# The first layer's prologue in quarters of the features: squares added on VectorE, roots by columns of tokens, first products in a new order

## The chip, the core and the metric

The kernel runs on one core of one Trainium2 chip. The metric is the device time of one execution in microseconds (us); the time given is the median of several executions. Its engines are TensorE (matrix products, PE in the rows, its weight loads PEld), VectorE (DVE), ScalarE (ACT), GpSimd (POOL) and SyncE (SP), each of which works through its own list of instructions in order; semaphores tie the lists together.

## What is computed

Two blocks run one after the other on 512 tokens of 1024 features. The change touches only the start of the first layer of the first block. Cut to that, the reference is:

```python
def rmsnorm(x, g):
    xf = x.astype(jnp.float32)
    y = xf * lax.rsqrt(jnp.mean(xf * xf, axis=-1, keepdims=True) + RMS_EPS)
    return (y * g.astype(jnp.float32)).astype(x.dtype)
def modulate(h, shift, scale):
    return h * (1 + scale) + shift
# first_block, layer 0: x is 512x1024, ctx 256x1024
shift, scale, gate = jnp.split(sc @ mod_w[l] + mod_b[l], 3, axis=-1)      # sc = silu(c)
hx = modulate(rmsnorm(x, norm_g[l]), shift[:, None], scale[:, None])
shift_c, scale_c, gate_c = jnp.split(scc @ mod_w[l] + mod_b[l], 3, axis=-1)   # scc = silu(c_ctx)
hc = modulate(rmsnorm(ctx, norm_g[l]), shift_c, scale_c)
# even mixer: z = h @ w_in, split into va, vg, ga, xb, gb
# conformer: u = va * sigmoid(vg), convolution, layernorm, silu, times silu(ga)
# recurrence: xb through a short convolution u; gates r, i from u; a scan; the context gives its start
```

## The kernel before

Everything is held feature-major: a tile is 128 features (partitions) by 512 tokens of x, or by 256 tokens of the context (`TC`), and there are `NT` = 8 tiles of features. A product runs in three passes over split numbers: `three` (L1781) issues w_hi times h_hi, w_hi times h_lo and w_lo times h_hi for one tile k, `blocks` runs over k. The weights come in chunks of 128x1024 in the order that `chunk_names` (L61) gives. Each chunk c passes through rings of `RING` = 4 buffers: a transfer into `raw` (SP's queue, the first ones ScalarE's), `w_hi` by ScalarE (`hi`, L473), `w_lo` by VectorE (`lo`, L1015). `ahead(name)` makes the part of the chunk `AHEAD` = 3 places further on. A product waits with `ready` for its w_lo (semaphore `lo`), and counts itself done on `mm`. The order of each engine is written out by hand in `act`, `dve`, `pe`, `sp` and `pool`; no planner moves anything.

The prologue has four parts.

1. Loads: on ScalarE's queue x in two halves, the context, then `modr` (shift and scale columns of `mod_w`) in four quarters of 2 MB each in the order `GROUPS`, three weight chunks ahead of the third quarter.
2. Roots: ScalarE squares the tiles (L530), VectorE adds them in pairs (`square_pair`, L1104), four matmuls with a matrix of ones (`first_sum`, L1834) sum over features and leave the sum on all partitions, ScalarE takes the root of 128x512 and 128x256, VectorE the reciprocals (L1053).
3. Conditioning: TensorE multiplies silu(c) by each quarter (`mod_rows`, L1819, 16 matmuls), ScalarE copies the rows out (`rows_copy`, L538), TensorE turns them into columns (`mod_columns`, L1827), VectorE makes gains out of them (`first_gains`, L1133 and L1136), once for each half of the features.
4. h: for each tile VectorE multiplies x, gain and reciprocal root (`first_tile`, L1144), ScalarE adds the shift and rounds (`first_high`, L544: `h_hi`, `hc_hi`), VectorE makes the low part (`first_low`, L1150).

`first_products` (L1849) then multiplies by halves: the context's product xc(0), then the gate vg(0) and the value va(0) together, tile by tile. Eight passes i follow: vg(i), va(i), xc(i+1) and gc(i), the last being the recurrence's gates of the context. For pass i ScalarE takes tanh of vg(i), and after gc(i) the gate functions (`head_gates`) and their roots; VectorE makes `U` (L1227), the short convolution (`head_conv`), the scan's inputs and the scan (`head_drive`, `head_scan`), and one column of the conditioning (`conditioning`, L1061) for later use. The low parts of the next chunks stand between them in the same list.

## Time and profile before

| | |
|---|---|
| time, median of 3 executions | 1636.33 us (1633.75, 1636.33, 1636.61) |
| profiled execution | 1635.51 us, its span 1634.2 us |
| granted TensorE clock, mean | 0.993 |
| busy: TensorE, VectorE, ScalarE | 1597.6, 978.5, 752.7 us |

The span is what the engines' records cover; the 1.3 us to the execution's own time lie around it. The granted clock is the TensorE clock that the chip allowed, as a share of full speed: 1.00 is 2.4 GHz, 0.50 is 1.2 GHz. In a timeline a row gives the start in us from the span's beginning, the duration, the engine, the source line, the operation with its output and inputs by name, and in brackets the idle time before it with what ended it. A row with x16 groups sixteen such instructions. Source lines are those of the kernel before.

### The profile page before, as it was taken

The numbers are of one execution on the slowest core, as the hardware profiler recorded it, in microseconds if no ns is written. First come the engines' busy times: TensorE is split into PE (matmuls) and PEld (weight loads), VectorE is DVE, ScalarE is ACT, GpSimd is POOL, SyncE is SP. The second block draws the span as 40 slices with busy tenths as digits, with TensorE's granted clock in tenths as the row PEclk, the third lists the DMA queues.
The fourth block names the chain that finished last, engine by engine and source line by source line (L and its number), as shares of the span: only waits on it lengthen the run. The fifth ranks groups of instructions, "written<-read, shape, count | busy, mean of one in ns | idle before, by whom it ended". The sixth has DMA issues, their size and how long they took to land.

```text
span 1634.2 us, 19145 instructions
## 1 busy us (share of the span) xinstructions
PE 1597.6 (98%) x7642; PEld 1272.4 (78%) x7642; DVE 978.5 (60%) x1421; ACT 752.7 (46%) x1050; POOL 23.7 (1%) x44
## 2 busy tenths in 40 slices
PE   5999999999999999999999989999999999999998
PEld 2888767677788888888878866787888888888886
DVE  5877778787886566645755544465456544444223
ACT  4788665755554333333355654345334333333212
POOL 0000000000000000000000000000000000000000
PEclk9999999999999999999999999999999999999999
DMA  9344456563233322333212211222223323223321
GB/s 390 128 144 170 154 194 190 192 193 128 92 102 103 103 92 90 103 104 96 94 54 91 68 62 52 90 78 77 91 90 103 103 91 103 91 94 99 103 90 52
DMA packets 54104, 185.75 MB, mean 114 GB/s; under 512 B 7392, under 2 KB 7392, under 8 KB 53120
## 3 DMA queue, kind: packets, MB, share of 16 engines
q1 hardware_dynamic: 47472, 152.70, 29.1%
q0 software_dynamic: 5104, 18.72, 3.6%
q10 hardware_dynamic: 1440, 13.11, 1.9%
q8 instruction: 60, 0.98, 0.2%
q14 instruction: 28, 0.23, 0.0%
HBM read 173.91 MB, written 2.10 MB: 108 GB/s over the span
## 4 chain that ended last, share of the span: by engine, by line
PE 89%; DVE 5%; ACT 2%; DMA 2%; issue 1%; ACTq 0%; DVEq 0%
PE banks L1784 24%; PE banks L1785 24%; PE banks L1786 24%; PE banks L1919 3%; PE banks L2288 2%; PE banks L2290 2%; PE banks L2289 2%; DMA mod<-modr 2%; DVE w_lo L1015 1%; PE banks L2129 1%; ACT w_hi L473 1%; PE banks L2143 1%; PE banks L2177 0%; PE banks L1803 0%; PE banks L2083 0%
## 5 line engine op out<-in xcount | busy, mean ns | idle before, releaser
L1784 PE MATMUL banks<-h_hi,w_hi 128*128 128x512 f32 x1344 | 530.4, 395 | 4.8 <-DVE M L1553 2.7
L1785 PE MATMUL banks<-h_lo,w_hi 128*128 128x512 f32 x1344 | 525.1, 391 | 0.0
L1786 PE MATMUL banks<-h_hi,w_lo 128*128 128x512 f32 x1344 | 524.9, 391 | 0.0
L1015 DVE TENSOR_TENSOR w_lo<-raw,w_hi 128x1024 fp32r<-128x1024 f32 (+1 forms) x274 | 324.7, 1192 | 265.7 <-ACT w_hi L473 265.2
L473 ACT ACTIVATE w_hi<-raw 128x1024 fp32r<-128x1024 f32 (+1 forms) x274 | 280.2, 1026 | 159.6 <-PE banks L2290 76.9
L1784 PEld LDWEIGHTS banks<-h_hi,w_hi 128*128 128x128 f32 x1344 | 253.5, 189 | 67.2 <-issue 9.1
L1786 PEld LDWEIGHTS banks<-h_hi,w_lo 128*128 128x128 f32 x1344 | 253.4, 189 | 54.0
L1785 PEld LDWEIGHTS banks<-h_lo,w_hi 128*128 128x128 f32 x1344 | 253.5, 189 | 51.1 <-issue 0.2
L1784 PE MATMUL banks<-y_hi,w_hi 128*128 128x512 f32 x192 | 75.4, 393 | 0.0
L1786 PE MATMUL banks<-y_hi,w_lo 128*128 128x512 f32 x192 | 74.7, 389 | 0.0
L1785 PE MATMUL banks<-y_lo,w_hi 128*128 128x512 f32 x192 | 74.7, 389 | 0.0
L2288 PE MATMUL banks<-w_hi,f_hi 128*128 128x512 f32 x176 | 68.6, 390 | 0.4 <-DVE w_lo L1015 0.4
L2289 PE MATMUL banks<-w_lo,f_hi 128*128 128x512 f32 x176 | 68.5, 389 | 0.0
L2290 PE MATMUL banks<-w_hi,f_lo 128*128 128x512 f32 x176 | 68.5, 389 | 0.0
L1919 PE MATMUL banks<-rep,raw 128*32 128x512 f32 x512 | 56.8, 595 | 0.0
L1751 DVE TENSOR_TENSOR fs<-banks,fs 128x512 f32<-128x512 f32 x22 | 15.2, 692 | 53.6 <-PE banks L1786 52.9
L991 ACT ACTIVATE f_hi<-fs 128x512 fp32r<-128x512 f32 x22 | 13.9, 632 | 70.9 <-DVE fs L1753 70.9
L1919 PEld LDWEIGHTS banks<-rep,raw 128*32 128x32 f32 x512 | 16.0, 109 | 36.4 <-issue 36.4
L1387 DVE TENSOR_TENSOR lev<-lev 128x632 f32<-128x632 f32 (+3 forms) x40 | 31.6, 790 | 20.4 <-ACT lev L718 19.5
L1784 PEld LDWEIGHTS banks<-y_hi,w_hi 128*128 128x128 f32 x192 | 36.0, 188 | 8.4 <-issue 0.9
L1786 PEld LDWEIGHTS banks<-y_hi,w_lo 128*128 128x128 f32 x192 | 36.0, 188 | 7.6
L1785 PEld LDWEIGHTS banks<-y_lo,w_hi 128*128 128x128 f32 x192 | 36.1, 188 | 7.3
(411 smaller groups left out, 2237.3 us busy)
## 6 DMA issues: line engine op xcount, KB each, us to landing
raw<-weights SPq DMA_DIRECT2D x263, 512.0 KB, 3.5
mraw<-modt POOLq DMA_DIRECT2D x32, 512.0 KB, 4.1
mod<-modr ACTq DMA_DIRECT2D x4, 2048.0 KB, 22.4
rep<-U SPq DMA_DIRECT2D x96, 64.9 KB, 2.4
raw<-weights SPq DMA_DIRECT2D x16, 256.0 KB, 3.2
rep<-U SPq DMA_DIRECT2D x32, 64.8 KB, 2.1
X<-x_in ACTq DMA_DIRECT2D x2, 1024.0 KB, 6.6
out<-Xt SPq DMA_DIRECT2D x8, 256.0 KB, 2.0
```

The lines of the kernel that those rows point to most:

```text
L473: fn(slot(w_hi, c, 0, WIDTH[c]), slot(raw, c, 0, WIDTH[c]), ACT.Copy).then_inc(S["hi"], 1)
L1015: tt(slot(w_lo, c, 0, w), slot(raw, c, 0, w), slot(w_hi, c, 0, w).bitcast(F32), ALU.subtract).then_inc(S["lo"], 1)
L1387: own.did(tt(here[:, :, wn // 2:wn // 2 + n], below[:, :, shift0:shift0 + n], below[:, :, shift0 + wn // 2:shift0 + wn // 2 + n], ALU.add))
L1784: mm(o, wh, r_hi, start=start, stop=False)
L1785: mm(o, wh, r_lo, start=False, stop=False)
L1786: return mm(o, wl, r_hi, start=False, stop=stop)
L1919: last = mm(banks[32 * j:32 * j + 32, 3 * 512:4 * 512], slot(raw, c, (8 * j + step) * 32, 32), rep[i % 2][:, a:a + T], start=step == 0, st ...
L2129: last = mm(banks[p0:p0 + HD, OUT * 512 + n * P:(OUT + 1) * 512], v[:, n * 256 + h * HD:n * 256 + (h + 1) * HD], w(n), start=n == 0, stop= ...
L2143: last = mm(pblk(n), kk[:, n * P:(n + 1) * P], q[:, n * P:T], start=True, stop=True)
L2288: mm(bank(g), lh, wh, start=k == 0, stop=False)
L2289: mm(bank(g), lh, wl, start=False, stop=False)
L2290: return mm(bank(g), ll, wh, start=False, stop=stop)
```

## The change

- The features are taken in four quarters of two tiles each instead of two halves. `modr` is laid out so that a quarter holds shift and scale of the same 256 features; all rows of the conditioning go through one bank. The loads of four weight chunks stand between those of the quarters.
- Squares of x are all added up on VectorE (seven additions, then seven for the context) instead of in pairs, and the sum over features is by columns of tokens: `token_sum` gives 128x4 and 128x2, roots and reciprocals work on these, and VectorE makes diagonal matrices of them, which TensorE spreads to all partitions (`first_spread`). The work on `lam` (softplus) moves ahead of the additions. `PREP` gives the count that each step reaches on the semaphore `x_prep`.
- `first_tile` multiplies x by its roots only (`xn`, the context in place), without waiting for gains. ScalarE then makes `n_t` and `h_hi`, both with gain and shift. In the last quarter VectorE makes its own `n_t` of x (`own_shift`).
- Chunks and products are in a new order: vg(0), va(0), xc(0), xc(1), vg(1), gc(0), then va(1), xc(2), gc(1), vg(2) and so on. The conditioning's rows 2 and 3 (`mod_rows`) and its columns stand between the first products. The w_hi and w_lo of vg(1) are made at the end of the prologue.

```diff
-GROUPS = (0, 2, 1, 3)
-ROWS_BANK = (2, 3, 5, 7)
+QUARTERS = 4
...
-    s = []
-    s += [("xc", 0)]
-    for i in range(NT):
-        s += [("vg", i), ("va", i)] + [("xc", i + 1)] * (i < NT - 1) + [("gc", i)]
+    s = [("vg", 0), ("va", 0), ("xc", 0), ("xc", 1), ("vg", 1), ("gc", 0)]
+    for i in range(1, NT):
+        s += [("vg", i)] * (i > 1) + [("va", i)] + [("xc", i + 1)] * (i < NT - 1) + [("gc", i)]
...
+    def own_shift(n):
+        return n // 4 == QUARTERS - 1 and first[n][0] == 1
...
-    first = [(q, k) for half in range(2) for q in range(2) for k in range(4 * half, 4 * half + 4)]
+    first = [(q, k) for j in range(QUARTERS) for q in (1, 0) for k in (2 * j, 2 * j + 1)]
...
-        for j, g in enumerate(GROUPS):
-            if j == 2:
-                for c in range(AHEAD):
-                    e.dma_start(slot(raw, c), wts[c, :, :]).then_inc(s_raw[c], 16)
-            e.dma_start(mod0[:, j * 4 * CW:(j + 1) * 4 * CW], modr[g, :, :]).then_inc(s_mod0[j], 16)
+        for j in range(QUARTERS):
+            e.dma_start(mod0[:, j * 4 * CW:(j + 1) * 4 * CW], modr[j, :, :]).then_inc(s_mod0[j], 16)
+            for c in ((0, 1), (2,), (3,), ())[j]:
+                e.dma_start(slot(raw, c), wts[c, :, :]).then_inc(s_raw[c], 16)
...
+            if n > 3:
+                e.wait_ge(S["x_prep"], PREP["add", 1, n - 3])
+            fn(square_of(n), tile(X, n), ACT.Square).then_inc(S["x_sq"], 1)
+        e.wait_ge(S["ctx"], 16)
+        for n in range(NT):
+            fn(tile(csq, n, TC), tile(ctx_x, n, TC), ACT.Square).then_inc(S["x_sq"], 1)
+        e.wait_ge(S["x_sum"], 1)
+        fn(rc0[:, 0:NB], bank(0, NB), ACT.Sqrt, bias=eps_rms, scale=1.0 / D).then_inc(S["f_sq"], 1)
+        e.wait_ge(S["x_sum"], 3)
+        fn(rc0[:, NB:NB + 2], bank(1, 2), ACT.Sqrt, bias=eps_rms, scale=1.0 / D).then_inc(S["f_sq"], 1)
...
+            src, w, hi_t, gain = ((ctx_x, TC, hc_hi, g0c), (xn, T, h_hi, g0))[q]
+            shift = modv0[:, 2 * k + 1 - q:2 * k + 2 - q]
+            e.wait_ge(S["x_prep"], PREP["times", q, k])
+            if n > 2:
+                e.wait_ge(S["norm_lo"], n - 2)
+            if not own_shift(n):
+                fn(n_t[n % 3][:, 0:w], tile(src, k, w), ACT.Identity, bias=shift, scale=gain[:, k:k + 1])
+            fn(tile(hi_t, k, w), tile(src, k, w), ACT.Identity, bias=shift, scale=gain[:, k:k + 1]).then_inc(S["norm_hi"], 1)
...
+        for j in range(QUARTERS):
+            e.wait_ge(S["norm_t"], 4 * j + 4)
+            for n in range(4 * j, 4 * j + 4):
+                first_high(n)
+                if j < QUARTERS - 1 and n % 4 == (1, 3, 1)[j]:
+                    rows_copy(j + 1)
+            if j < 2:
+                hi(2 + j)
         e.wait_ge(S["crep"], 16)
         fn(csb[:, :], csb[:, :], ACT.Silu).then_inc(S["csb"], 1)
-        for n in range(8, 16):
-            first_high(n)
...
+        def gate(i):
+            product("vg", i)
+            if i:
+                e.wait_ge(S["uu"], i)
+            fn(tg[:, :], bank(1), ACT.Tanh, scale=0.5).then_inc(S["sig"], 1)
...
-                head_input(i + 1, 4)
+                head_input(i + 1, (4, 7)[(i + 1) % 2])
+            if i == 0:
+                ahead("vg", 1)
+                gate(1)
             ahead("gc", i)
             product("gc", i)
             head_gates(i, [bank(5, TC), bank(5, TC, TC), bank(6, TC), bank(6, TC, TC)])
...
+        def square_sum(q, k):
+            e.wait_ge(S["x_sq"], NT * (1 - q) + k + 1)
+            a, b = (square_of(0), square_of(k)) if q else (tile(csq, 0, TC), tile(csq, k, TC))
+            if k > 1:
+                e.wait_ge(S["x_prep"], PREP["add", q, k - 1])
+            tt(a, a, b, ALU.add).then_inc(S["x_prep"], 1)
...
+        def diagonals(n, o, w):
+            e.wait_ge(S["f_sq"], n)
+            own.did(e.reciprocal(rc0[:, o:o + w], rc0[:, o:o + w]))
+            own.wait()
+            for j in range(o, o + w):
+                ts(tile(xdg, j, P), ident, rc0[:, j:j + 1], None, ALU.mult).then_inc(S["x_prep"], 1)
...
+        for k in range(1, NT):
+            square_sum(1, k)
+        for k in range(1, 6):
+            square_sum(0, k)
+        e.wait_ge(S["cst"], 16)
+        diagonals(1, 0, NB)
+        for k in (6, 7):
+            square_sum(0, k)
+        def first_gains(j):
+            e.wait_ge(S["cols"], j + 1)
...
+            e.wait_ge(S["x_sum"], 2 if q else 4)
+            if q:
+                tt(tile(xn, k), tile(X, k), bank(2), ALU.mult).then_inc(S["x_prep"], 1)
+            else:
+                tt(tile(ctx_x, k, TC), tile(ctx_x, k, TC), bank(3, TC), ALU.mult).then_inc(S["x_prep"], 1)
...
+            if own_shift(n):
+                e.wait_ge(S["norm_lo"], n - 2)
+                e.wait_ge(S["norm_t"], 4 * QUARTERS)
+                own.did(ts(n_t[n % 3][:, :], tile(xn, k), g0[:, k:k + 1], modv0[:, 2 * k:2 * k + 1], ALU.mult, ALU.add))
+                own.wait()
             e.wait_ge(S["norm_hi"], n + 1)
...
+            low(tile(lo_t, k, w), n_t[n % 3][:, 0:w], tile(hi_t, k, w)).then_inc(S["norm_lo"], 1)
+        first_tile(0)
+        first_tile(1)
+        diagonals(2, NB, 2)
+        first_tile(2)
+        first_tile(3)
+        for j in range(QUARTERS):
+            first_gains(j)
+            for n in range(4 * j, 4 * j + 4):
+                first_low(n)
+                if j == 0 and n < 2:
+                    lo(n)
+                if j == 1 and n % 4 > 1:
+                    lo(n % 4)
+                if j < 3:
+                    first_tile(4 + n)
+        ahead("va", 0)
...
         for i in range(NT):
-            ahead("vg", i)
-            ahead("va", i)
+            if i > 1:
+                ahead("vg", i)
+            if i:
+                ahead("va", i)
             e.wait_ge(S["sig"], i + 1)
             product("va", i)
             stt(tile(U, i, T, UW, UW + HALO), tg[:, :], 1.0, bank(0), ALU.add, ALU.mult).then_inc(S["uu"], 1)
+            if i == 0:
+                ahead("xc", 0)
+                head_conv(0)
+                head_low(0)
             if i < NT - 1:
                 ahead("xc", i + 1)
                 head_conv(i + 1)
+            if i == 0:
+                ahead("vg", 1)
             ahead("gc", i)
...
+        e.wait_ge(S["x_prep"], PREP["add", 1, NT - 1])
+        token_sum(0, square_of(0), s_one, True, True).then_inc(S["x_sum"], 1)
         e.wait_ge(S["sil"], 1)
         mod_rows(0)
+        first_spread(2, 0, NB)
+        e.wait_ge(S["x_prep"], PREP["add", 0, NT - 1])
+        token_sum(1, tile(csq, 0, TC), s_one, True, True, 2).then_inc(S["x_sum"], 1)
+        mod_columns(0)
+        first_spread(3, NB, 2)
         mod_rows(1)
-        mod_columns(0)
         mod_columns(1)
...
+        def first_gate(k, names=("vg", "va")):
+            e.wait_ge(S["norm_lo"], place[1, k] + 1)
+            for name in names:
+                if k == 0:
+                    ready(name, 0)
+                last = three(bank((0, 1)[name == "vg"]), C[name, 0], k, tile(h_hi, k), tile(h_lo, k), k == 0, k == KC - 1)
+                if k == KC - 1:
+                    last.then_inc(S["mm"], 1)
+        def first_context(i, j):
+            for k in (2 * j, 2 * j + 1):
+                e.wait_ge(S["norm_lo"], place[0, k] + 1)
+                if k == 0:
+                    ready("xc", i)
+                last = three(bank((4, 7)[i], TC), C["xc", i], k, tile(hc_hi, k, TC), tile(hc_lo, k, TC), k == 0, k == KC - 1)
+            if k == KC - 1:
+                last.then_inc(S["mm"], 1)
+        first_gate(0)
+        first_gate(1)
+        first_gate(2)
         mod_rows(2)
+        first_gate(3)
+        mod_columns(2)
+        first_context(0, 0)
+        first_context(0, 1)
         mod_rows(3)
...
+        first_context(1, 0)
+        first_context(1, 1)
+        first_gate(4)
+        mod_columns(3)
+        first_gate(5)
+        first_context(0, 2)
+        first_context(1, 2)
+        for name in ("vg", "va"):
+            first_gate(6, (name,))
+            first_gate(7, (name,))
+        first_context(0, 3)
+        first_context(1, 3)
...
+            if i > 1:
                 c = ready("vg", i)
                 e.wait_ge(S["sig"], i)
                 blocks(bank(1), c, h_hi, h_lo).then_inc(S["mm"], 1)
+            if i:
                 c = ready("va", i)
                 e.wait_ge(S["uu"], i)
                 blocks(bank(0), c, h_hi, h_lo).then_inc(S["mm"], 1)
-            if i < NT - 1:
+            if 0 < i < NT - 1:
                 c = ready("xc", i + 1)
-                e.wait_ge(S["xp"], i + 1)
-                blocks(bank(4, TC), c, hc_hi, hc_lo, w=TC).then_inc(S["mm"], 1)
+                e.wait_ge(S["xp"], i)
+                blocks(bank((4, 7)[(i + 1) % 2], TC), c, hc_hi, hc_lo, w=TC).then_inc(S["mm"], 1)
...
+            if i == 0:
+                c = ready("vg", 1)
+                e.wait_ge(S["sig"], 1)
+                blocks(bank(1), c, h_hi, h_lo).then_inc(S["mm"], 1)
...
+    modr = a["mod_w"][0][:, :2 * D].reshape(KC, P, 2, QUARTERS, T // 2).transpose(3, 1, 0, 2, 4).reshape(QUARTERS, P, KC * T)
```

**TensorE in the prologue.** Before, from the columns of the first two quarters to the first product; L1819 are the conditioning's rows, L1827 its columns, L1784 to L1786 the products:

```order
L1827 MATMUL banks<-vec,rows_86 128x2 [waits s_rows_c]
L1827 MATMUL banks<-vec,rows_86 128x2 x3
L1819 MATMUL banks<-mod_83,csum 32x512 [waits s_mod0_2]
L1819 MATMUL banks<-mod_83,csum 32x512 x7
L1819 MATMUL banks<-mod_83,csum 32x512 [waits s_mod0_3]
L1819 MATMUL banks<-mod_83,csum 32x512 x7
L1784 MATMUL banks<-hc_hi,w_hi 128x256 [waits s_lo,s_norm_lo]
L1785 MATMUL banks<-hc_lo,w_hi 128x256
```

After, from the value's half of gate 2 (the products of vg(0) and va(0) with tile 2 of x) to the columns of the third quarter; L1870 are the rows, L1835 to L1837 the products:

```order
L1835 MATMUL banks<-h_hi,w_hi 128x512
L1836 MATMUL banks<-h_lo,w_hi 128x512
L1837 MATMUL banks<-h_hi,w_lo 128x512
L1870 MATMUL banks<-mod_83,csum 32x512 [waits s_mod0_2]
L1870 MATMUL banks<-mod_83,csum 32x512 x7
L1835 MATMUL banks<-h_hi,w_hi 128x512 [waits s_norm_lo]
L1836 MATMUL banks<-h_lo,w_hi 128x512
L1837 MATMUL banks<-h_hi,w_lo 128x512
L1835 MATMUL banks<-h_hi,w_hi 128x512
L1836 MATMUL banks<-h_lo,w_hi 128x512
L1837 MATMUL banks<-h_hi,w_lo 128x512
L1878 MATMUL banks<-vec,rows_89 128x2 [waits s_rows_c]
```

The rows of the third quarter stood ahead of every product; now three gates stand ahead of them, and gate 3 ahead of their columns. The products of x come ahead of those of the context.

**VectorE in the prologue.** After, between the gains of the first quarter (L1169) and those of the second (L1166); L1177 and L1179 multiply x and the context by their roots, L1048 makes a low part of h, L1039 one of a weight:

```order
L1169 SCALAR_TENSOR_TENSOR small<-small,vec 128x2 [waits s_norm_t]
L1169 SCALAR_TENSOR_TENSOR small<-small,vec 128x2
L1048 TENSOR_TENSOR h_lo<-n_t_90,h_hi 128x512 [waits s_norm_hi]
L1039 TENSOR_TENSOR w_lo<-raw,w_hi 128x1024 [waits s_hi]
L1177 TENSOR_TENSOR xn<-X,banks 128x512 [waits s_x_sum]
L1048 TENSOR_TENSOR h_lo<-n_t_91,h_hi 128x512 [waits s_norm_hi]
L1039 TENSOR_TENSOR w_lo<-raw,w_hi 128x1024 [waits s_hi]
L1177 TENSOR_TENSOR xn<-X,banks 128x512 [waits s_x_sum]
L1048 TENSOR_TENSOR hc_lo<-n_t_92,hc_hi 128x256 [waits s_norm_hi]
L1179 TENSOR_TENSOR ctx_x<-ctx_x,banks 128x256 [waits s_x_sum]
L1048 TENSOR_TENSOR hc_lo<-n_t_90,hc_hi 128x256 [waits s_norm_hi]
L1179 TENSOR_TENSOR ctx_x<-ctx_x,banks 128x256 [waits s_x_sum]
```

Before, the gains come once for four tiles, and each product with the roots takes the gain in the same instruction.

**TensorE in the second pass.** Before, the end of gc(0) and what follows it, vg(1):

```order
L1784 MATMUL banks<-u_hi,w_hi 128x256
L1785 MATMUL banks<-u_lo,w_hi 128x256
L1786 MATMUL banks<-u_hi,w_lo 128x256
L1784 MATMUL banks<-h_hi,w_hi 128x512 [waits s_sig,s_lo]
L1785 MATMUL banks<-h_lo,w_hi 128x512
L1786 MATMUL banks<-h_hi,w_lo 128x512
```

After, the end of gc(0) and what follows it, va(1):

```order
L1835 MATMUL banks<-u_hi,w_hi 128x256
L1836 MATMUL banks<-u_lo,w_hi 128x256
L1837 MATMUL banks<-u_hi,w_lo 128x256
L1835 MATMUL banks<-h_hi,w_hi 128x512 [waits s_uu,s_lo]
L1836 MATMUL banks<-h_lo,w_hi 128x512
L1837 MATMUL banks<-h_hi,w_lo 128x512
```

The product vg(1) moved from behind gc(0) to ahead of it.

**VectorE in the second pass.** Before, the end of the scan of pass 0 (L1203, L1237), the conditioning's column (L1061) and the low parts of gc(1) and vg(2):

```order
L1195 TENSOR_TENSOR ti_76<-ti_76,th_80 128x256 [waits s_v,s_sq]
L1203 SCALAR_TENSOR_TENSOR tr_74<-aa_78,ti_76 128x256 [waits s_v]
L1237 COPY small<-tr_73 128x1 [waits s_v]
L1237 COPY small<-tr_74 128x1
L1061 ISA mraw,modcol<-mraw,csb 128x1024 [waits s_csb,s_mraw0]
L1061 ISA modcol 128x1
L1015 TENSOR_TENSOR w_lo<-raw,w_hi 128x512 [waits s_hi]
L1015 TENSOR_TENSOR w_lo<-raw,w_hi 128x1024 [waits s_hi]
L1227 SCALAR_TENSOR_TENSOR U<-tg,banks 128x512 [waits s_mm,s_sig]
```

After, the same stretch, with the low part of vg(2) at L1039:

```order
L1241 TENSOR_TENSOR ti_76<-ti_76,th_80 128x256 [waits s_v,s_sq]
L1249 SCALAR_TENSOR_TENSOR tr_74<-aa_78,ti_76 128x256 [waits s_v]
L1288 COPY small<-tr_73 128x1 [waits s_v]
L1288 COPY small<-tr_74 128x1
L1085 ISA mraw,modcol<-mraw,csb 128x1024 [waits s_csb,s_mraw0]
L1085 ISA modcol 128x1
L1039 TENSOR_TENSOR w_lo<-raw,w_hi 128x1024 [waits s_hi]
L1272 SCALAR_TENSOR_TENSOR U<-tg,banks 128x512 [waits s_mm,s_sig]
```

The list there is the same but for the low part of 128x512, that of gc(1), which now stands ahead of `head_drive(0)`.

## Rows read from the trace of the kernel before

**Rows 1.** The busy line: busy us, share of the span, instructions.

```profile
PE 1597.6 (98%) x7642; PEld 1272.4 (78%) x7642; DVE 978.5 (60%) x1421; ACT 752.7 (46%) x1050; POOL 23.7 (1%) x44
```

**Rows 2.** TensorE's waits, 0 to 130 us: us in total, times, longest.

```profile
PE banks L1819 <- DMA mod<-modr: 2.6, 1, 2.6
PE banks L1784 <- DVE w_lo L1015: 0.8, 1, 0.8
PE banks L1784 <- DVE h_lo L1150: 0.7, 1, 0.7
```

**Rows 3.** TensorE's timeline, 30 to 40 us: start, us, engine, line, operation, idle before.

```profile
30.46 1.95 PE L1827 MATMUL banks<-vec,rows 128*128 128x2 f32 x16
...
32.34 1.93 PE L1819 MATMUL banks<-mod,csum 128*32 128x512 f32 x16
...
36.85 2.58 PE L1819 MATMUL banks<-mod,csum 128*32 128x512 f32 x16 [2.58 <-DMA mod<-modr]
...
39.35 0.58 PE L1784 MATMUL banks<-hc_hi,w_hi 128*128 128x256 f32 x1
```

**Rows 4.** ScalarE's exponential, VectorE's softplus work and additions, 9 to 20 us.

```profile
9.19 0.22 ACT L521 ACTIVATE small<-small 128x16 f32<-128x16 f32 x1
...
12.13 0.17 DVE L1032 TENSOR_SCALAR small<-small 128x16 f32<-128x16 f32 x1
...
15.80 0.68 DVE L1104 TENSOR_TENSOR aa<-aa,aa 128x512 f32<-128x512 f32 x1
...
19.47 0.43 DVE L1104 TENSOR_TENSOR aa<-aa,aa 128x256 f32<-128x256 f32 x1 [2.38 <-ACT aa L530]
```

**Rows 5.** A later norm's sum by columns and four diagonals, timeline at 475 us.

```profile
474.90 0.95 PE L1803 MATMUL banks<-small,s 128*128 128x1 f32 x8
...
476.39 0.88 DVE L1069 TENSOR_SCALAR rstd_b<-cst,small 128x128 f32<-128x128 f32 x4
```

**Rows 6.** VectorE's timeline, 29 to 33 us: weight low parts, first gains.

```profile
29.84 2.36 DVE L1015 TENSOR_TENSOR w_lo<-raw,w_hi 128x1024 fp32r<-128x1024 f32 x2
...
32.45 0.24 DVE L1133 TENSOR_TENSOR small<-banks,vec 128x8 f32<-128x8 f32 x2 [0.25 <-PE banks L1827]
```

**Rows 7.** ScalarE's groups by form: busy us, mean ns of one; idle before, releaser.

```profile
L473 ACT ACTIVATE w_hi<-raw 128x1024 fp32r<-128x1024 f32 x258 | 270.4, 1052 | 159.6 <-PE banks L2290 76.9 <-PE banks L1786 76.3 <-PE banks L2085 4.7
...
L599 ACT ACTIVATE aa<-tr,small 128x512 f32<-128x512 f32 x16 | 13.1, 820 | 0.0
...
L544 ACT ACTIVATE h_hi<-n_t,small 128x512 fp32r<-128x512 f32 x8 | 5.7, 721 | 3.6 <-DVE n_t L1144 3.6
...
L538 ACT ACTIVATE rows<-banks 128x512 f32<-128x512 f32 x4 | 2.4, 592 | 4.1 <-PE banks L1819 4.1
```

**Rows 8.** ScalarE's timeline, 44 to 47 us: table load and silu.

```profile
44.23 1.28 ACT L559 ACT_TABLE_LOAD   x1
...
45.53 1.06 ACT L559 ACTIVATE csb<-csb 128x1024 f32<-128x1024 f32 x1
```

**Rows 9.** Timeline, 62 to 78 us: vg(1), va(1), low parts, vg(2).

```profile
62.54 0.40 PE L1784 MATMUL banks<-h_hi,w_hi 128*128 128x512 f32 x1
...
68.00 0.39 PE L1784 MATMUL banks<-h_hi,w_hi 128*128 128x512 f32 x1
...
74.48 1.82 DVE L1015 TENSOR_TENSOR w_lo<-raw,w_hi 128x512 fp32r<-128x512 f32 x2
...
77.76 0.40 PE L1784 MATMUL banks<-h_hi,w_hi 128*128 128x512 f32 x1
```

**Rows 10.** TensorE's timeline, 996 to 1001 us, after an idle time.

```profile
996.95 0.61 PE L1784 MATMUL banks<-h_hi,w_hi 128*128 128x512 f32 x1 [2.73 <-DVE M L1553]
...
1000.67 0.39 PE L1784 MATMUL banks<-h_hi,w_hi 128*128 128x512 f32 x1
```

**Rows 11.** Two windows: each engine's busy us; last three: TensorE clock, DMA share, GB/s.

```profile
38.00:40.00 2.00, 2.00 (x11) 0.65 (x4) 1.15 (x3) 0.53 (x2) 0.00 (x0) 0.50 1.00 385
998.00:1000.00 2.00, 2.00 (x6) 1.54 (x6) 1.97 (x8) 0.00 (x0) 0.00 (x0) 0.50 0.47 184
```

167 lines of the change are left out of this document (49 added, 118 removed).

## Prediction

> **What bounds the kernel now.** I read the busy line first [rows 1]: TensorE is busy for 98% of the span, so outside the start the time is TensorE's work, and a microsecond in which it idles is lost. The start is the exception, and the change lies there. Of TensorE's waits in the first 130 us [rows 2], three stand after the sums of squares: 2.6 us for the last quarter of the conditioning's matrix (its load ends at 36.8), 0.7 for a low part of h, 0.8 for a low weight part. TensorE's timeline shows the order [rows 3]: the third quarter of the conditioning's rows at 32.34, the last at 36.85 after its wait, the first product at 39.35. From there TensorE runs all but dense. So two things count: how much product work TensorE has behind it when it becomes dense, and which idle time comes later.
>
> **Squares and roots.** The softplus work now stands ahead of the additions on VectorE. It took 12.13 to 15.80, 3.7 us, and can begin when ScalarE's exponential ends, 9.4 [rows 4]: done at 13.1. Seven additions of 128x512 follow, each on the sum of the last, so without overlap: 7 x 0.68, 17.9. Five on the context at 0.43: 20.1. The first roots come a little later, over ScalarE: its last square of x waits for the fourth addition (15.8), then 0.6 for it, as for a copy of that size [rows 7], eight context squares of half the size at about 0.3, the table load of 1.3 [rows 8] and 0.3 for the root, 20.5. The reciprocal takes 0.2 (with the root that is the 0.5 between the two rows of [rows 5]), four diagonals 0.9: 21.7. The last two additions: 22.6. These replace reciprocals of 128x512 and 128x256. Then a chain over three engines: the context's sum, half of the 0.95 of [rows 5], its root, a w_hi of 1.05 and a copy of the rows of 0.59 [rows 7] that ScalarE issues between (with the root 2.0), four column matmuls (half of 1.95 [rows 3]), two diagonals spread 0.5, two context tiles 0.8, the gains 0.5 [rows 6]: 22.6 + 0.5 + 2.0 + 0.9 + 0.5 + 0.8 + 0.5 = 27.8. Gate k, below, is the products of vg(0) and va(0) with the k-th tile of x. The first stands behind the second quarter's columns, whose rows ScalarE copies after two pairs of 128x512 (3.0): 27.8 + 3.0 + 0.6 + 0.9 = 32.3.
>
> **The first two quarters.** ScalarE makes n_t and h_hi from xn with scale and bias both read from memory. The trace has that form at 0.82 for 128x512, against 0.72 with a bias alone [rows 7]; one starts about 0.1 before its forerunner ends, so the pair takes 1.5: h_hi(0) at 29.3. Then VectorE's order decides. Between the first low part and the second quarter's gains stand three more low parts, four products of x with its roots and two w_lo: two at 2.36 together [rows 6], four operations of 128x512 at 0.6 (0.69 less the overlap), four of 128x256 at 0.35, 6.1 in all: 35.4. Gains 0.5, a pair on ScalarE 1.5, a low part 0.7: the second quarter's first product starts at 38.1 by this, and some tenths later with the handovers between engines, which I left out; I take **38.6**. TensorE has by then done only the gates of the first two tiles of x, with gaps.
>
> **TensorE's account of the prologue.** At 38.6 it is 0.75 ahead of 39.35. It has 12 products of 128x512 behind it: 24 take 68.00 - 62.54 = 5.46 [rows 9], so 2.7. It still owes the conditioning's rows of quarters 3 and 4, which before were paid while loads were waited for: 2 x 1.93 [rows 3] = 3.9. Sum: 0.4 behind. Idle time after that: before 0.7 + 0.8 [rows 2]. After, gates 6 and 7 wait for their own shifted tiles, up to 1.0. The product vg(1) now needs its w_hi behind four context operations of 0.5, a table load of 1.28 [rows 8], a silu and the w_hi itself of about 1.0 each, and a w_lo of 1.2, after the last gains and two high parts (1.4): 7.8 us. TensorE's own way from these gains is 1.7 for the first low part, 0.5 for the second, 2.7 for twelve products and 1.4 for twelve of the context: 6.3. It waits 1.5. Together 2.5 against 1.5: 1.0 worse. **The prologue loses 1.4 us**, I say 1.5. The granted clock is taken as no difference: at 38 to 40 it is 0.50 before [rows 11] after 2.6 of idle time, and after has some 2 us without work ahead of gate 2. If it stays up, about 0.9 comes back (half of the 2 us of work that stood at 0.50 from 39.35 on); if the low stretch is longer or a quarter later, up to 1.5 more is lost.
>
> The last load costs nothing in either: rows of quarter 4 are now wanted at about 45, behind gates and contexts, and the load, with one weight chunk of 0.5 MB more ahead of it and the silu's input behind it, ends within 1 us of 36.8.
>
> **What the new order costs in the second pass.** This is the largest term. vg(1) now stands ahead of gc(0). ScalarE's and VectorE's work on pass 0 (gate functions, roots, scans, the conditioning's column) begins when gc(0) ends and is not shortened. In before gc(0) is over at 62.54 and VectorE comes free at 74.48, 11.9 us later, to make the w_lo of gc(1) and of vg(2) [rows 9]. These were done at 76.3, and vg(2) began at 77.76: hidden by 1.5. After, TensorE has between gc(0) and vg(2) only va(1), xc(2) and gc(1): 77.76 - 68.00 = 9.8. The w_lo of vg(2) is ready at 11.9 + 1.2 + 0.1 = 13.2. **TensorE waits 3.4 us.** Its cover, the 5.5 us of vg(1), is gone. It can't be recovered: the following passes are as dense as before. Bounds: 0, if VectorE somehow reaches it earlier, and 4.0, if ScalarE comes 0.5 late to gc(0) because tanh of vg(1) and two w_hi stand in front.
>
> An idle time like this also costs clock. After 2.73 us of it at 994, TensorE runs at the lower of its two levels until 1000.67 [rows 10], granted clock 0.50 [rows 11]: nine products of 128x512 start in that time, 3.7 instead of 9 x 0.23 = 2.05, **1.7 us**. Bounds: 0 (the idle times of 0.7 and 0.8 show no fall) and 2.1. 3.4 is nearer to 2.73, so I take 1.7.
>
> **Sum.** 1.5 + 3.4 + 1.7 = 6.6 us later. The profiled execution took 1635.5, 0.8 below the median of 1636.3 and within the runs' 1633.75 to 1636.6: **1642.1**, and I give 1642.
>
> A rule of the Trainium skill, *ScalarE: Activation LUTs*, section What ACT_TABLE_LOAD costs, speaks further against the change: a switch of tables costs about 2.66 us, a load of 1.28 and a drain of 1.38. The row of the silu's load shows 1.28, and its activation follows at 45.53, 1.30 after the load began [rows 8], so this trace does not show the drain. By the rule the wait of vg(1) would be 1.4 longer and the time about 1643.5.
>
> **Rivals.** *The prologue pays in full* (ends faster). Place: 32.3 to 46, where TensorE could run from the first gate without a gap, if VectorE handed over each quarter as fast as it is used. Price: 7.0 earlier, less 3.9 for rows, and 0.9 of clock and 1.5 of idle time back: 5.5 gained. It decides if gate 2 starts before 35. For: the load wait of 2.6 is truly filled, and the long reciprocals are gone. Against: the walk over VectorE gives 38.6, and the second pass then takes 5.1 back, 1635.1; faster by more than can be told only if its wait is missing as well: 1630.0.
>
> *The second pass hides it.* If the 11.9 us shrinks or the w_lo comes in time, only the prologue is left: 1637. Against it: same instructions, same engines.
>
> *The clock stays up in both places*: 1.7 and 0.9 less, 1639.5.
>
> *The quarters come slower.* Each of the four passes through ScalarE and VectorE in series, and the idle ends at rows_copy(2), which waits behind ScalarE's quarter; one us more in each: 1646.
>
> **How the numbers follow.** Forecast of 1639.6 to 1644.5: 0.67. Clock stays up, 1639.5: 0.08, half of it within 0.2%. Hidden second pass, 1637: 0.09. Prologue in full with the stall, 1635.1: 0.05; without it, 1630.0: 0.04. Slower quarters, 1646: 0.07. With 0.2% (3.3 us, about what a measurement of this kernel can tell) around 1636.3: faster 0.05 (0.04 and some rest), same 0.18 (0.09, 0.05, 0.04), slower 0.77. The range 1637 to 1646 leaves out what lies below 1637, about 0.12, and little above.
>
> **What would show it.** TensorE: idle of 3 to 4 us before vg(2), released by w_lo, at 77 to 82, then granted clock 0.5. Gate 2 at 38 to 39.5 with 1 to 2.5 idle before it, released by h_lo. A wait of 1 to 2 us for w_lo before vg(1). No wait for the load of quarter 4. gc(0) starting at 66 to 68 instead of 61. Wrong if vg(2) follows gc(1) without a gap, or gate 2 starts before 36.

## The result and the profile after

The changed kernel takes **1646.01 us** (median of 4 executions, 1643.36 to 1649.04), the kernel before 1635.99 in the same comparison: ratio 1.0064, 95% interval 1.0049 to 1.0079. It is 10 us slower. The forecast was 5.7 us slower; its direction was right and each loss stood where it was forecast, but two of its terms were too small.

Apart from two slow executions of the kernel before (1792 and 3429 us, left out of every ratio), the executions of one kernel differ by up to 6 us, and the granted clock goes with them: the changed kernel's fastest was 1643.36 at a mean clock of 0.994, its slowest 1649.04 at 0.990. The profiled execution is the slowest of its four (span 1647.7 against 1634.2). So below, small effects are read off landmarks in the traces, and the whole time only confirms the large ones. A landmark is one product that both kernels have; how much later it starts than in the kernel before is the loss up to there.

The page's busy line of the changed kernel, against [rows 1]:

```profile
PE 1599.8 (97%) x7650; PEld 1276.7 (77%) x7650; DVE 978.9 (59%) x1443; ACT 760.6 (46%) x1064; POOL 23.7 (1%) x44
```

TensorE has 2.2 us more to do and 11.3 more in which it does nothing. Its waits in the first 130 us, against [rows 2]:

```profile
PE banks L1854 <- DVE aa L1141: 20.7, 1, 20.7
PE banks L1835 <- DVE w_lo L1039: 5.2, 2, 3.7
PE banks L1878 <- ACT rows L549: 3.4, 2, 1.8
PE banks L1835 <- DVE h_lo L1048: 1.2, 1, 1.2
```

The wait for the last quarter's load (2.6) is gone. The two of w_lo are those of vg(1) and vg(2). The first row is new: TensorE does nothing at all until 20.7; before, it was summing squares from 11.3 on. Its timeline through the prologue, against [rows 3] (start, us, then engine, line and operation):

```profile
20.70 1.84 PE L1854 MATMUL banks<-small,aa 128*128 128x1 f32 x8 [20.70 <-DVE aa L1141]
22.47 3.64 PE L1870 MATMUL banks<-mod,csum 128*32 128x512 f32 x16
26.04 1.93 PE L1886 MATMUL banks<-xdg,cst 128*128 128x128 f32 x8
27.81 0.50 PE L1854 MATMUL banks<-small,csq 128*128 128x1 f32 x4
...
37.74 0.61 PE L1835 MATMUL banks<-h_hi,w_hi 128*128 128x512 f32 x1
...
43.75 0.51 PE L1835 MATMUL banks<-h_hi,w_hi 128*128 128x512 f32 x1 [1.25 <-DVE h_lo L1048]
...
65.66 0.50 PE L1835 MATMUL banks<-h_hi,w_hi 128*128 128x512 f32 x1 [1.51 <-DVE w_lo L1039]
```

The same sixteen matmuls of a quarter's rows that took 1.93 in [rows 3] take 3.64, as they do in e6 (below) at a granted clock of 0.50. So by their duration they run at the lower of TensorE's two levels, after 20.7 us without work. The granted clock doesn't show it there: in this trace it reads 1.00 until 31.2 us, 0.50 from 31.2 to 34.5, 1.00 until 38 and 0.50 again until 41.4. Gate 0 starts at 37.74 (forecast 32.3), gate 2 at 43.75 (38.6), and vg(1) waits 1.51 (1.5).

The second pass, TensorE and VectorE, against [rows 9] and [rows 10]: the last product of gc(1), the low part of vg(2), and vg(2) itself until the clock is back; then the clock by windows (the value ahead of the DMA share):

```profile
82.32 0.28 PE L1837 MATMUL banks<-u_hi,w_lo 128*128 128x256 f32 x1
86.32 0.79 PE L1835 MATMUL banks<-h_hi,w_hi 128*128 128x512 f32 x1 [3.71 <-DVE w_lo L1039]
...
92.74 0.40 PE L1835 MATMUL banks<-h_hi,w_hi 128*128 128x512 f32 x1
```

```profile
85.04 1.22 DVE L1039 TENSOR_TENSOR w_lo<-raw,w_hi 128x1024 fp32r<-128x1024 f32 x1
```

```profile
86.00:90.00 4.00, 3.68 (x9) 2.91 (x10) 3.89 (x8) 3.99 (x11) 0.00 (x0) 0.50 0.84 292
90.00:92.00 2.00, 2.00 (x6) 1.54 (x5) 2.00 (x5) 1.98 (x4) 0.00 (x0) 0.50 0.53 211
92.00:94.00 2.00, 2.00 (x9) 1.60 (x8) 1.86 (x6) 1.97 (x5) 0.00 (x0) 0.86 0.84 238
```

The stall that was forecast stands where it was forecast, 3.71 us (forecast 3.4), released by that low part. The products behind it run at 0.50 for 6.4 us (86.32 to 92.74), not 3.7.

**The account.** The same product in both traces gives the loss so far. The last product of gc(1) starts at 77.64 before and at 82.32 after: the prologue with the first pass costs **4.68**. The first product of xc(3) starts at 88.67 before and at 100.27 after, 11.60 later: the second pass adds **6.92**, of which 3.71 is the stall and the rest, 3.2, the clock (half of the 6.4). In the profiled execution another 1.9 come later, most of them in a low stretch at 799 us that the trace of before does not have at that point (see the last section). The median holds 10.0 of this; that the low stretches fall differently in the other executions is likely but not shown, since only one has a trace.

### The profile page after: what moved, and what is told of

It is laid out like the page before. It is cut to its first block, busy times and chain, and to the rows that moved or that the text cites. A ratio compares the mean times of both kernels' runs of the same rounds, so it can differ in the third digit from the quotient of the medians.

```text
span 1647.7 us, 19223 instructions
## 1 busy us (share of the span) xinstructions
PE 1599.8 (97%) x7650; PEld 1276.7 (77%) x7650; DVE 978.9 (59%) x1443; ACT 760.6 (46%) x1064; POOL 23.7 (1%) x44
## 4 chain that ended last, share of the span: by engine, by line
PE 88%; DVE 6%; ACT 3%; issue 2%; ACTq 0%; DVEq 0%
PE banks L1835 24%; PE banks L1837 24%; PE banks L1836 24%; PE banks L1999 3%; PE banks L2368 2%; PE banks L2370 2%; PE banks L2369 2%; DVE w_lo L1039 1%; ACT w_hi L488 1%; PE banks L2209 1%; PE banks L2223 1%; PE banks L1854 1%; PE banks L2257 0%; PE banks L2163 0%; PE banks L2165 0%
## 5 line engine op out<-in xcount | busy, mean ns | idle before, releaser
L1835 PE MATMUL banks<-h_hi,w_hi 128*128 128x512 f32 x1344 | 533.3, 397 | 10.5 <-DVE w_lo L1039 5.2
L1837 PE MATMUL banks<-h_hi,w_lo 128*128 128x512 f32 x1344 | 526.8, 392 | 0.0
L1039 DVE TENSOR_TENSOR w_lo<-raw,w_hi 128x1024 fp32r<-128x1024 f32 (+1 forms) x274 | 325.1, 1192 | 270.3 <-ACT w_hi L488 269.7
L1835 PEld LDWEIGHTS banks<-h_hi,w_hi 128*128 128x128 f32 x1344 | 254.5, 189 | 75.2 <-issue 9.9
L1837 PEld LDWEIGHTS banks<-h_hi,w_lo 128*128 128x128 f32 x1344 | 254.7, 189 | 54.4
L1835 PE MATMUL banks<-y_hi,w_hi 128*128 128x512 f32 x192 | 75.4, 393 | 0.0
L1837 PE MATMUL banks<-y_hi,w_lo 128*128 128x512 f32 x192 | 74.8, 390 | 0.0
L1835 PEld LDWEIGHTS banks<-y_hi,w_hi 128*128 128x128 f32 x192 | 36.1, 188 | 8.3 <-issue 0.9
L1837 PEld LDWEIGHTS banks<-y_hi,w_lo 128*128 128x128 f32 x192 | 36.1, 188 | 7.6
```

What stands on the lines that cost most here:

```text
L1039: tt(slot(w_lo, c, 0, w), slot(raw, c, 0, w), slot(w_hi, c, 0, w).bitcast(F32), ALU.subtract).then_inc(S["lo"], 1)
L1835: mm(o, wh, r_hi, start=start, stop=False)
L1837: return mm(o, wl, r_hi, start=False, stop=stop)
```

## The experiments

b1 is an edit of the kernel before, the others of the changed kernel; c2 combines several edits, and c3a, c3 and c4 build on c2. The landmarks are given as us later than in the kernel before: the last product of gc(1), the first of xc(3) and the last of gc(2). A ratio is against the kernel before on the same chip; the kernel before's medians there were 1634.5 to 1636.1, so ratios are compared and not medians.

| kernel | median us | ratio, 95% interval | end of gc(1) | start of xc(3) | end of gc(2) |
|---|---|---|---|---|---|
| the change | 1646.01 | 1.0064 (1.0049 to 1.0079) | 4.68 | 11.60 | 11.60 |
| e1_late_issue | 1645.97 | 1.0067 (1.0054 to 1.0079) | 3.22 | 9.98 | 9.98 |
| e2_early_low | 1640.51 | 1.0035 (1.0023 to 1.0048) | 5.15 | 5.15 | 5.87 |
| e3_rows_first | 1645.30 | 1.0063 (1.0050 to 1.0075) | 3.50 | 10.34 | 10.34 |
| e4_silu_late | 1643.66 | 1.0056 (1.0042 to 1.0070) | 4.64 | 9.74 | 9.74 |
| e5_old_second_pass | 1646.72 | 1.0063 (1.0050 to 1.0075) | 11.56 | 11.56 | 11.56 |
| e6_warm | 1643.56 | 1.0048 (1.0033 to 1.0063) | 3.11 | 8.66 | 8.66 |
| e7_silu_last | 1646.57 | 1.0058 (1.0046 to 1.0071) | 4.68 | 11.35 | 11.35 |
| b1_before_eleven | 1636.00 | 1.0009 (1.0000 to 1.0018) | 0.81 | 0.81 | 0.81 |
| c2_combined | 1638.20 | 1.0012 (1.0003 to 1.0021) | 3.14 | 3.14 | 3.84 |
| c3a_rows_earlier | 1636.53 | 1.0009 (1.0000 to 1.0018) | 2.56 | 2.56 | 3.27 |
| c3_rows_and_low | 1635.26 | 1.0004 (0.9996 to 1.0013) | 1.09 | 1.09 | 1.81 |
| c4_own_shift | 1635.74 | 1.0000 (0.9991 to 1.0009) | -0.59 | -0.60 | 0.12 |

From the end of gc(2) on the distance stays the same in every kernel for at least 100 us more, so the last column is what the start costs.

### Why the prologue starts late

ScalarE's own queue and its first functions in the changed kernel:

```profile
5.74 0.46 ACTq L524 DMA_DIRECT2D raw<-weights  x1
6.23 1.83 ACTq L522 DMA_DIRECT2D mod<-modr  x1
...
8.15 1.28 ACT L527 ACT_TABLE_LOAD   x1 [8.15 <-issue]
```

The same in the kernel before:

```profile
5.08 0.97 ACTq L513 DMA_DIRECT2D mod<-modr  x2
6.14 1.28 ACT L516 ACT_TABLE_LOAD   x1 [6.14 <-issue]
```

The changed kernel has one transfer more on that queue, and the eleventh issue takes 1.83 us where the others take 0.4 to 0.7. **e1_late_issue**:

```diff
-        for j in range(QUARTERS):
+        for j in range(QUARTERS - 1):
...
+        e.dma_start(mod0[:, 12 * CW:16 * CW], modr[3, :, :]).then_inc(s_mod0[3], 16)
         for n in range(NT):
             if n % 4 == 0:
```

> Edit to the changed kernel: the issue of the last quarter of modr, the eleventh transfer on ScalarE's queue, stands behind the exponential instead of ahead of ScalarE's first function. Theory A (in the changed kernel the issue of that transfer holds ScalarE: 1.83 us at 6.23, and its first table load begins at 8.15 instead of 6.14, so the whole chain of squares, sums and roots starts 2.0 us late, and everything up to the first dense stretch moves with it): first table load at about 6.3, exponential at 9.3 instead of 11.17, gate 2 at about 42 instead of 43.75, time 1.5 to 2 us below the changed kernel's 1646.0, so about 1644.3. Rival B (the start of the first gates is set by loads of the conditioning or by TensorE's order, not by ScalarE's start): the exponential moves, gate 2 stays at 43.7, time 1646. Rival C (the queue blocks whenever an eleventh transfer is issued): the issue takes 1.8 us at its new place too and the first square starts at 11.2 all the same; time 1646.

```profile
6.41 1.28 ACT L527 ACT_TABLE_LOAD   x1 [6.41 <-issue]
7.96 0.22 ACT L527 ACTIVATE csum<-vec 128x8 f32<-128x8 f32 x1 [0.26 <-DMA vec<-vecs]
...
8.42 0.33 ACTq L533 DMA_DIRECT2D mod<-modr  x1
9.69 0.21 ACT L532 ACTIVATE small<-small 128x16 f32<-128x16 f32 x1
```

Issued two microseconds later, the same transfer takes 0.33: C falls. The exponential comes 1.48 earlier (9.69 for 11.17; the load of vec now ends last), gate 2 too (42.28), and gc(1) 1.46: A holds in the trace, B does not. The ratio did not move (1.0067 for 1.0064); 1.5 us is less than what executions differ by.

**b1_before_eleven** does the same thing alone to the kernel before, in the other direction:

```diff
             e.dma_start(mod0[:, j * 4 * CW:(j + 1) * 4 * CW], modr[g, :, :]).then_inc(s_mod0[j], 16)
+            if j == 2:
+                e.dma_start(slot(raw, AHEAD), wts[AHEAD, :, :]).then_inc(s_raw[AHEAD], 16)
...
-        for c in range(AHEAD, N_CHUNKS):
+        for c in range(RING, N_CHUNKS):
```

> Edit to the kernel before: the fourth weight chunk is loaded on ScalarE's queue, between the last two quarters of modr, instead of on SP's; ScalarE's queue so has eleven transfers ahead of its first function, as in the changed kernel, and nothing else changes. Theory A (the eleventh issue holds ScalarE: in the changed kernel it took 1.8 us): the last issue takes 1.5 to 2.0 us, ScalarE's first table load begins at about 8.1 instead of 6.14 and its exponential at 11.2; the first product, which waits for the last load, comes about 1.2 later, with that load's 0.5 MB more ahead of it, at 40.5; time 1 to 1.5 us above the kernel before. Rival B (in the changed kernel ScalarE was late for a semaphore or for vec, not for the queue): table load at 6.2 to 6.8, the issue under 1 us.

```profile
6.34 1.56 ACTq L513 DMA_DIRECT2D mod<-modr  x1
7.99 1.28 ACT L518 ACT_TABLE_LOAD   x1 [7.99 <-issue]
```

The eleventh issue takes 1.56 and ScalarE starts 1.85 later. A holds, in the time too: 1.0009, 1.5 us. The 0.81 at the landmarks is not the price of the late start alone: TensorE waits for the last load in this kernel (2.57 us), and that load now has 0.5 MB more ahead of it.

**e3_rows_first** and **e6_warm** take up TensorE's lower level. The first:

```diff
+        e.wait_ge(S["sil"], 1)
+        mod_rows(0)
         e.wait_ge(S["x_prep"], PREP["add", 1, NT - 1])
         token_sum(0, square_of(0), s_one, True, True).then_inc(S["x_sum"], 1)
-        e.wait_ge(S["sil"], 1)
-        mod_rows(0)
```

> Edit to the changed kernel: TensorE multiplies the first quarter of the conditioning ahead of the sum over x's tokens instead of behind it. Theory A (in the changed kernel TensorE does nothing until 20.70, then takes 3.64 us for that product at the lower clock, and the context's sum, ready at 25.3, is not issued until 27.81): the rows run from about 17 to 20.7, the context's sum starts at about 25.4 and gate 2 at about 41.5 to 42.5 instead of 43.75; time about 1.5 us less than 1646.0. Rival B (VectorE's and ScalarE's passes over the tiles alone set gate 2): less than 0.5 us. Rival C (the first quarter is not loaded before 20.7): the sum over x's tokens is held up, and the time is above 1646.

The second:

```diff
+        for k in range(1, 6):
+            e.wait_ge(S["x_prep"], PREP["add", 1, k])
+            mm(bank(7, 256), ones, cst[:, 0:256], start=True, stop=True)
         e.wait_ge(S["x_prep"], PREP["add", 1, NT - 1])
```

> Edit to the changed kernel: five more matmuls of ones by constants, 128x256, on TensorE while it waits for the sums of squares, one behind each of VectorE's first five additions, into a bank that is used later; their result goes nowhere. Theory A (in the changed kernel TensorE is idle until 20.70, and its work from there to 41.4 runs at the lower of its two levels for lack of work ahead: the first quarter's rows take 3.64 us instead of 1.93, the spread 1.93 instead of 0.95): the rows take 1.9 to 2.4, the context's sum starts at about 25.6 instead of 27.81, gate 2 at 41.5 to 42.5 instead of 43.75; end of gc(1) 1.5 us earlier. Rival B (the clock there does not depend on such work): nothing moves.

TensorE with the five extra matmuls (their result goes nowhere):

```profile
21.80 1.92 PE L1870 MATMUL banks<-mod,csum 128*32 128x512 f32 x16
23.66 1.16 PE L1886 MATMUL banks<-xdg,cst 128*128 128x128 f32 x8
25.36 0.61 PE L1854 MATMUL banks<-small,csq 128*128 128x1 f32 x4 [0.55 <-DVE csq L1141]
...
30.48 3.64 PE L1870 MATMUL banks<-mod,csum 128*32 128x512 f32 x16
```

With work ahead of them the rows take 1.92 instead of 3.64, and the context's sum starts at 25.36, when it is ready, instead of 27.81. Gate 2 comes at 42.16 (1.6 earlier), gc(1) 1.57 earlier. The low level is not gone but later: the second quarter's rows take 3.64 here for 3.11, at a granted clock of 0.50 from 28 to 34 us, so of the 2.45 us gained at the context's sum 1.6 arrive. With the rows moved (e3) gate 2 starts at 42.54, and gc(1) comes 1.18 earlier. There the clock is not the reason: the spread takes 2.08 and the second quarter's rows 3.07, at 0.50. The rows no longer stand ahead of the context's sum, which starts at 25.21. A holds for both in the traces; the ratios, 1.0063 and 1.0048, can't tell it.

### The second pass

**e2_early_low**, on ScalarE and on VectorE:

```diff
-            if i:
+            if i > 1:
                 ahead("va", i)
...
             product("gc", i)
+            if i == 0:
+                ahead("va", 1)
             head_gates(i, [bank(5, TC), bank(5, TC, TC), bank(6, TC), bank(6, TC, TC)])
...
-            if i:
                 ahead("va", i)
...
             ahead("gc", i)
+            if i == 0:
+                ahead("va", 1)
             head_drive(i)
```

> Edit to the changed kernel: w_hi and w_lo of vg(2) are made as soon as gc(0) is over, ahead of pass 0's gate functions on ScalarE and ahead of the scan's inputs on VectorE. Theory A (TensorE's 3.7 us of idle time ahead of vg(2) is that low part's place behind pass 0's work in the two lists): no wait ahead of vg(2), granted clock 1.00 behind it, 3.7 of idle time and 1.7 to 3.4 of clock come back, time about 1640 (1639 to 1641). Rival B (pass 0's work is itself late for pass 1, so that the wait only moves, to va(2) or gc(1)): a new wait of 1 us or more on U or u_lo and 2 us or less gained.

```profile
74.25 2.96 DVE L1041 TENSOR_TENSOR w_lo<-raw,w_hi 128x1024 fp32r<-128x1024 f32 x3
```

```profile
84.00:92.00 8.00, 8.00 (x37) 6.60 (x36) 7.86 (x16) 7.67 (x14) 0.53 (x1) 1.00 0.47 138
```

The three low parts, that of vg(2) the last, are done at 77.2; in the changed kernel vg(2)'s was done at 86.3. No wait is left there and the clock is 1.00 from 84 to 92. From the end of gc(1) to xc(3) nothing is lost any more (5.15 and 5.15), against 6.92. A small part moved: the end of gc(1) is 0.47 later than in the changed kernel, and behind xc(3) there is a wait ahead of gc(2), whose low part stands behind the scan and the conditioning's column of pass 1:

```profile
97.31 0.38 PE L1838 MATMUL banks<-u_hi,w_hi 128*128 128x256 f32 x1 [0.47 <-DVE w_lo L1041]
```

The kernel before and the changed kernel have no wait there. So 5.73 us have come back at the end of gc(2) (11.60 less 5.87); the ratio fell from 1.0064 to 1.0035, 4.7 us. A holds; B, with a new wait of 1 us or more, does not. It is the most valuable edit, and a small one.

**e5_old_second_pass** puts gc(0) ahead of vg(1) again, in the order of the chunks (shown) and in each engine's list:

```diff
-    s = [("vg", 0), ("va", 0), ("xc", 0), ("xc", 1), ("vg", 1), ("gc", 0)]
+    s = [("vg", 0), ("va", 0), ("xc", 0), ("xc", 1), ("gc", 0)]
     for i in range(1, NT):
-        s += [("vg", i)] * (i > 1) + [("va", i)] + [("xc", i + 1)] * (i < NT - 1) + [("gc", i)]
+        s += [("vg", i)] + [("va", i)] + [("xc", i + 1)] * (i < NT - 1) + [("gc", i)]
```

> Edit to the changed kernel: the chunk vg(1) and its product stand behind gc(0) again, as in the kernel before; everything of the prologue stays changed. Theory A (the wait of 3.7 us ahead of vg(2) comes from moving vg(1) ahead of gc(0)): no wait ahead of vg(2); in its place gc(0) waits for the short convolution and u_lo of pass 0, which vg(1) covered: about 3 us (copy 0.37, four steps of 0.4, u_hi and u_lo 0.4 each after xc(0) ends at 63, with the silu of csb ahead on ScalarE), with part of the clock. Time 1642 to 1645. Rival B (the wait ahead of vg(2) comes from the late prologue, not from the order): a wait of 3 us or more ahead of vg(2) stays, time 1646 or more.

```profile
70.51 0.55 PE L1829 MATMUL banks<-u_hi,w_hi 128*128 128x256 f32 x1 [6.29 <-DVE u_lo L1045]
```

Theory A is half right. The wait ahead of vg(2) is gone, so it is the order that puts it there, and B fails; but gc(0) now waits 6.29 for u_lo, twice what was expected, and the loss at xc(3) is the same 11.56. The move of vg(1) was no mistake in itself: with the new prologue, in which xc(0) and vg(0) both end last, something has to cover the short convolution. What was missing was the low part's move that belongs to it.

**e4_silu_late** and **e7_silu_last** attack the wait of 1.51 ahead of vg(1). The first puts `ahead("va", 0)` on ScalarE ahead of the silu of csb, the second `gate(0)`, the tanh, as well (the edit shown is the second's):

```diff
-        e.wait_ge(S["crep"], 16)
-        fn(csb[:, :], csb[:, :], ACT.Silu).then_inc(S["csb"], 1)
...
         ahead("va", 0)
         gate(0)
+        e.wait_ge(S["crep"], 16)
+        fn(csb[:, :], csb[:, :], ACT.Silu).then_inc(S["csb"], 1)
```

> Edit to the changed kernel: on ScalarE the w_hi of vg(1) stands ahead of the table load and the silu of csb instead of behind them. Theory A (the wait of 1.51 us ahead of vg(1) is these 2.3 us on ScalarE): no wait there, w_lo of vg(1) done at about 63.6 instead of 65.6, time 1.5 us less than 1646.0, about 1644.5. Rival B (tanh of vg(0) or the second pass behind it takes it back): the wait ahead of vg(2) grows by as much, since gc(0)'s end and pass 0's work are tied to VectorE, and the time stays at 1646.

> Edit to the changed kernel: on ScalarE the w_hi of vg(1) and the tanh of vg(0) both stand ahead of the silu of csb. In the kernel with w_hi alone ahead of it the wait passed on to the tanh (1.34 us). Theory A (vg(1) needs both, and the silu with its table load is the whole of the wait): at most 0.3 us of wait ahead of vg(1), end of gc(1) 1.3 us earlier than in the changed kernel, the wait ahead of vg(2) 3.2 to 3.7 as before since gc(0) is earlier by as much, time 1643 to 1645. Rival B (the table load alone, 1.28 us, still has to stand ahead of the tanh): a wait of about 1 us stays.

In e4 the wait stays, 1.34 us, now for the tanh that reads the bank, and the end of gc(1) is where it was (4.64): neither of its theories holds. In e7, first TensorE, then ScalarE:

```profile
64.47 0.47 PE L1835 MATMUL banks<-h_hi,w_hi 128*128 128x512 f32 x1 [0.40 <-ACT tg L624]
70.89 0.36 PE L1835 MATMUL banks<-u_hi,w_hi 128*128 128x256 f32 x1 [0.71 <-DVE u_lo L1048]
```

```profile
62.44 1.28 ACT L624 ACT_TABLE_LOAD   x1
...
64.35 1.28 ACT L629 ACT_TABLE_LOAD   x1
65.64 1.06 ACT L629 ACTIVATE csb<-csb 128x1024 f32<-128x1024 f32 x1
```

vg(1) starts 1.19 earlier, then gc(0) waits 0.71 for u_lo and is only 0.34 earlier, and the end of gc(1) has not moved. Both of my theories for e7 fail too: the wait ahead of vg(1) was covered by the next one, that of the convolution, so removing it is worth nothing; the tanh ahead of the silu also costs a second table load, one that a silu had spared the tanh. e4's earlier xc(3) is mostly its clock: there the stretch at 0.50 is 3.4 us long, with a stall of 3.25 instead of 3.71. The length of the stall alone doesn't decide this: e6 has a stall of 3.68, and its stretch at 0.50 is 3.4 us long too (86.0 to 89.4).

### All of it together

**c2_combined** takes e1, e2, e3 and e7 together and orders the first two quarters' steps as early as their loads allow (TensorE's part of it):

```diff
         token_sum(0, square_of(0), s_one, True, True).then_inc(S["x_sum"], 1)
+        mod_columns(0)
         first_spread(2, 0, NB)
...
         token_sum(1, tile(csq, 0, TC), s_one, True, True, 2).then_inc(S["x_sum"], 1)
-        mod_columns(0)
+        mod_rows(1)
         first_spread(3, NB, 2)
-        mod_rows(1)
```

> Edits to the changed kernel together: last quarter of modr issued behind the exponential; first quarter's rows ahead of the sum over tokens; w_hi and tanh ahead of the silu of csb; w_hi and w_lo of vg(2) as soon as gc(0) is over; and the first two quarters' rows, copies and columns as early as their loads allow (rows_copy(0) behind the first root, its columns ahead of the spread, the second quarter's rows ahead of the context's spread, the first gains ahead of the second product by roots). Theory A (the price of the change lay in ScalarE's start, the low clock, the order of the first quarter's steps and the second pass's low part, which are all to be had back): first product at 29 to 31 instead of 37.74, gate 2 at 36 to 38, end of gc(1) at about 75 instead of 82, no wait ahead of vg(2), time 1631 to 1634, below the kernel before. Rival B (VectorE's and ScalarE's serial passes over four quarters set the end of the prologue): gate 0 comes early, but the waits move to gates 2, 4 and 6, and the end of gc(1) stays at or above the kernel before's; time 1635 to 1640.

The first product comes at 34.19, gate 2 at 41.05 and the end of gc(1) at 80.78. A fails. B is nearer: the first gate comes early, but the waits stand at gates 0, 1 and 2 (2.3, 1.3 and 0.4 us) and not at 2, 4 and 6, the first two for low parts of weights, at the lower level from 35.5 to 42.3.

**c3a_rows_earlier** moves the rows of quarters 3 and 4 into those waits, **c3_rows_and_low** also puts the low parts of the first two weight chunks and the gains of the second quarter earlier on VectorE, **c4_own_shift** also gives VectorE the shift of every tile of x. The three edits in one, cut:

```diff
         mod_columns(1)
+        mod_rows(2)
...
         first_gate(0)
         first_gate(1)
+        e.wait_ge(S["rows_c"], 3)
+        mod_rows(3)
         first_gate(2)
-        mod_rows(2)
+        mod_columns(2)
         first_gate(3)
...
         diagonals(2, NB, 2)
+        lo(0)
         first_tile(2)
         first_tile(3)
+        lo(1)
...
-        return n // 4 == QUARTERS - 1 and first[n][0] == 1
+        return first[n][0] == 1
```

> Edit to the combined kernel: on TensorE the third quarter's rows stand ahead of gate 0 and the fourth's between gates 1 and 2, where TensorE waited 2.3, 1.3 and 0.4 us, and ScalarE copies them out as early. Theory A (what the combined kernel still loses against the kernel before, 3.1 us at the end of gc(1), is rows paid in the dense stretch and work at the lower clock at 35.5 to 42.3): end of gc(1) 1.5 to 3.5 us earlier, time about 1635 to 1636.5. Rival B (the gates 2 and 3 wait for VectorE and start no earlier; only rows move, and the fourth quarter's load, at 37, holds gate 2 back): under 1 us gained.

> Edits to the combined kernel: the rows of quarters 3 and 4 as in the kernel beside it, and on VectorE the low parts of the first two weight chunks ahead of h's low parts and the gains of the second quarter ahead of the last low part of the first. Theory A (VectorE's order holds back gates 0, 1 and 2): gate 0 at 33 to 34, gate 1 without a wait, gate 2 at 38 to 39.5 instead of 41.05; end of gc(1) at 76 to 78, at or ahead of the kernel before; time 1633.5 to 1635.5. Rival B (the fourth quarter's load or ScalarE's pairs of 1.4 us now set gate 2): no better than the kernel beside it.

> Edit to the kernel with earlier rows and low parts: for every tile of x VectorE makes its own n_t (0.55 us) and ScalarE only h_hi, as the changed kernel does in its last quarter alone, so that each tile of x takes one operation of 0.80 on ScalarE instead of two. Theory A (the waits of 0.98 and 1.26 us for h_lo at the first gate of quarters 2 and 3 are ScalarE's pair, 1.4 us behind the gains): each of these waits falls below 0.5, gate 2 at 40.0 to 40.5 instead of 40.94, end of gc(1) 1.5 to 2.5 us earlier and at or ahead of the kernel before's; time 1633 to 1634.5. Rival B (VectorE is the engine that sets the quarters, and 0.55 more for each tile costs what ScalarE gives back): the waits stay within 0.3 us of what they were, time 1635.3 or more.

c3a gains only 0.6 at the end of gc(1): gate 2 waits 0.42 as it did and starts at 42.41 for 41.05, the rows having pushed the gates back (its B). c3 gains 2.05 over c2 and ends gc(1) at 78.73, short of A's 78, with gate 2 at 40.94, short of its 38 to 39.5. c4 gains another 1.7 there, within A's 1.5 to 2.5, with gate 2 at 39.52, but the time, 1635.74, is not in A's range, and one wait is above its 0.5. What is left in c4 of waits for h_lo:

```profile
34.22 0.50 PE L1846 MATMUL banks<-h_hi,w_hi 128*128 128x512 f32 x1 [0.17 <-DVE h_lo L1053]
...
47.56 0.50 PE L1846 MATMUL banks<-h_hi,w_hi 128*128 128x512 f32 x1 [0.62 <-DVE h_lo L1053]
...
53.33 0.50 PE L1846 MATMUL banks<-h_hi,w_hi 128*128 128x512 f32 x1 [0.40 <-DVE h_lo L1053]
...
54.51 0.50 PE L1846 MATMUL banks<-h_hi,w_hi 128*128 128x512 f32 x1 [0.22 <-DVE h_lo L1053]
```

c4 is 0.6 us ahead of the kernel before at the end of gc(1) and at xc(3), but the wait ahead of gc(2) that e2's move brings (0.46 here) costs 0.7 of it, and from there on c4 is 0.12 behind. Its time agrees: ratio 1.0000, interval 0.9991 to 1.0009. No version here beats the kernel before; the idea of the change, well ordered, comes out even. Whether w_lo of gc(2) can also be made earlier, and the 0.6 kept, was not tried.

## Why the prediction was wrong

- **Direction and rivals.** Slower, as forecast. None of the four rivals came true. The nearest is *the quarters come slower* (1646), by its number alone and so by luck: from gate 0 to gate 2 it took 6.0 us, forecast 6.3.
- **The second pass.** The stall is 3.71 for 3.4. The 11.9 us from the end of gc(0) to VectorE's being free were 12.4 (72.66 to 85.04). The mechanism is shown by e2 and, for the order, by e5. The stall was not unavoidable, though: "it can't be recovered" held for this order only, and I did not ask whether the low part itself could go first.
- **The clock behind the stall.** This is the first mis-sized term: 1.7 forecast, with an upper bound of 2.1, and 3.2 measured in the profiled execution. The duration was taken from one stretch of 3.7 us [rows 10]. The low stretch lasted 6.4 us here and 3.4 us in e4 and e6. One row gave one of the two values, and half the length of a low stretch, which is what it costs, has to be bounded by more than one such row.
- **The prologue.** The second and larger one: 1.5 forecast, 4.68 measured. My account of it held in form. With gate 2 at 43.75, TensorE is 4.4 late against 39.35; it has 2.7 behind it and owes 3.9, so 5.6; idle time afterwards is 1.5 in both; 0.9 comes back, since the clock is up from 43.75 on; that makes 4.7. The step that failed is gate 2's start, 5.15 too early, and it was so from gate 0 on (5.4).
- **Why gate 0 was late.** Three things were missing from the walk. I let the exponential end at 9.4, as before, and did not count the added transfer as an instruction of ScalarE's: 1.5 to 2.0 us (e1, b1). I took each of the seven additions for 0.68; every one waits for the sum before it, and they start 0.80 apart, 0.7 us in all. With both, the context's squares are added up at 25.3, forecast 22.6. And I took TensorE to be free and at full clock for the context's sum, issued at 27.81 instead: it stood behind rows and a spread at the lower level (e3, e6: 1.2 to 1.6 at the end of gc(1)). In gate 0 these are 2.0, 0.7 and 2.5 of 5.4; from there on the walk holds within 0.3. The 0.7 is read off the rows and was not tested by a run:

```profile
15.09 0.69 DVE L1141 TENSOR_TENSOR aa<-aa,aa 128x512 f32<-128x512 f32 x1
15.88 0.69 DVE L1141 TENSOR_TENSOR aa<-aa,sq 128x512 f32<-128x512 f32 x1
16.68 0.69 DVE L1141 TENSOR_TENSOR aa<-aa,tg 128x512 f32<-128x512 f32 x1
```

- **Smaller ones.** vg(1)'s wait was right to 0.01, with both of its sides 0.3 to 0.4 longer than given (8.1 and 6.7 us from the last gains for 7.8 and 6.3), and worth nothing (e7). Gates 6 and 7, given up to 1.0, waited for nothing. The low stretch at 38 to 41.4, which the prediction left open, stood over gates 0 and 1 ahead of a wait of 1.25, and the clock was back at gate 2; the low level that cost time was the one from 20.7 to 34.5.
- **The table load.** The silu's load took 1.28 and its function began 1.30 behind it once more (61.04 and 62.34), so the drain that the Trainium skill adds (*ScalarE: Activation LUTs*, What ACT_TABLE_LOAD costs) does not show here either, and the 1643.5 by that rule is nearer to the result only by chance.
- **The range.** Its upper end, 1646.0, was built from one microsecond more in the quarters; the two terms that were too small lay outside what it covered. With the 11.6 us of the trace the same sum gives 1647.1.

## What to carry to other kernels

A transfer that is added to a compute engine's queue is an instruction of that engine: count its issue in the engine's own chain, above all ahead of its first function. When work moves off TensorE at the start, ask what clock the next matmuls will see, and put real work that is already loaded into the gap, ahead of what others wait for; in e3 and e6 this gave 1.2 and 1.6 us, though the low level only came later. When a product is moved ahead of another, move the preparation of the product behind it too: here that was one call moved on each of two engines, and half of the loss (5.7 of 11.6). Then follow the trace past the place that was mended: the move brought a new wait of 0.5 us one product beyond the landmark.

## What the runs showed of the hardware

- The eleventh transfer issued on ScalarE's queue at 6.1 to 6.4 us took 1.55 to 1.99 us to issue in seven kernels (1.83 in the changed one) and, in the kernel before with one more (b1), 1.56; the ten ahead of it took 0.4 to 1.1 each, and the same transfer issued at 8.1 to 8.7 us in five kernels (e1 and the four combined ones) 0.33. Whether the count of transfers, their bytes or those not yet landed decides was not tried.
- TensorE's low level can come without idle time ahead of it. In the profiled execution of the changed kernel it was busy for 38.9 of 39 us and then ran at 0.52:

```profile
799.00:802.00 3.00, 3.00 (x12) 2.52 (x11) 2.63 (x4) 0.66 (x2) 0.00 (x0) 0.52 0.25 70
760.00:799.00 39.00, 38.91 (x191) 32.56 (x190) 17.24 (x27) 13.68 (x20) 0.55 (x1) 1.00 0.29 93
```

  Such stretches of 3.4 us stood at 787 to 799 in five of the traces (the change, e5, e7, c3, c4) and not in the others; others as long stood at 818 to 836 in seven, the kernel before among them. One costs 1.7 us where TensorE is busy throughout (half of its length). That they make up part of the 6 us between executions is an inference from the mean clocks (0.990 to 0.994), since each kernel has one trace; what sets them off stays open.
